# A four-layer hybrid decoder trunk on one core: the first two weight units split by halves, identity products before them, a padded input tensor, and three splits of weights in other places

## The chip, the cores and the metric

The kernel runs on one NeuronCore of one Trainium2 chip. TensorE (PE in the profile) multiplies, VectorE (DVE), ScalarE (ACT) and GpSimd (POOL) do the rest, and SyncE (SP) issues nearly all of the transfers. The metric is the device time of one execution in microseconds (us), as the median of several runs; lower is better.

## What is computed

256 tokens of width 1024 go through four layers. Each is a token mixer and an MLP, both behind an RMSNorm and with a residual. The mixers are latent attention (MLA, layers 0 and 3), block-sparse attention (MoBA, layer 1) and a Mamba-2 scan (SSD, layer 2).

```python
def reference(x, positions, ...):
    for i in range(4):
        h = rmsnorm(x, norm_mix[i])
        m = (mla_mixer, moba_mixer, ssd_mixer)[i % 3](h, ...)
        x = x + m
        x = x + sq_relu_mlp(rmsnorm(x, norm_mlp[i]), mlp_w1[i], mlp_w2[i])   # relu(h@w1)**2 @ w2
    return rmsnorm(x, norm_final)

def mla_mixer(h, positions, w_in, q_norm, w_uq, kv_norm, w_ukv, w_o):
    c_q, c_kv, k_pe = split(h @ w_in, [256, 512])            # w_in: 1024 x 576
    q = (rmsnorm(c_q, q_norm) @ w_uq)                        # 16 heads of 128 + 64
    k_nope, v = split(rmsnorm(c_kv, kv_norm) @ w_ukv)        # 16 heads of 128 + 128
    # rotary turn of q_pe and k_pe, causal softmax attention, then @ w_o
```

## The kernel before, in words

**Products in three parts.** Every fp32 operand is split into a high part (a rounded copy, type fp32r) and a low part (the value less its high part). A product a*b becomes three matmuls, a_hi*b_hi, a_hi*b_lo and a_lo*b_hi (`mm3`, lines 561 to 563). For the inputs the parts are `hhi` and `hlo`, both in the tile `hsplit`; for the weights they are `whi` and `wlo`. In the up-projections of the MLP (`pe_up`, lines 920 and 922) one matmul reads 512 columns, high and low part of `hsplit` side by side, and the next one 256.

**Weight units.** All weights come in 207 units of up to 128 x 2048 numbers (1 MB), in one fixed order (`units`), through four slots of `raw`, `whi` and `wlo`. SP loads unit n into `raw` (line 2075). ACT writes `whi` (`act_splits`, line 534), DVE writes `wlo` (`dve_splits`, line 544), and PE waits for that. SP may load slot s again when DVE has split it; ACT may write `whi` of slot s again when PE has used it. Each engine runs its own instruction list in program order; where in these lists the splits stand is written by hand: `act_splits(act, key, ahead)` and `dve_splits(dve, key, ahead)` emit all splits up to `ahead` units beyond `key`.

**The start.** The tokens are two tiles t = 0, 1 of 128. For each tile ACT sums the squares, DVE scales to a mean (`ms`, line 662), POOL takes the power -1/2 (`rstd`, line 745), DVE scales (`xn`, line 666), PE transposes (line 761), ACT writes `hhi` (line 611) and DVE `hlo` (line 688). Units 0 and 1 (the names `ca`, `cb` in `compress`) are the upper and lower half of the rows of the 1024 x 512 part of `w_in`; unit 2 holds the last 64 columns (`kpe`) and the first part of `w_uq`, unit 3 the first part of `w_ukv`, and units 4 and 5 the next parts of these two. PE runs `compress(0,0)`, then the transposes of tile 1, then `compress(1,0)`, `compress(0,1)` and `compress(1,1)`: 12 matmuls each, the first index is the unit, the second the tile. The latents that come out of them are normed too: ACT squares (`c_ssq`, line 1337), DVE `c_ms` (line 1382), POOL `c_rstd`, DVE writes the normed latents over `xn` (line 1389), and PE turns them (`turn(t)`, line 1256), with the 24 matmuls of `kpe` between the two turns. Behind the squares of tile 0, and in layer 0 alone, ACT computes the sines of the rotary angles (`act_angles`); DVE prepares them (`dve_turns`, `dve_angles`). Layer 3 goes the same way without the angles.

**The scan.** In the SSD layer a loop over q = 0 to 4 takes a quarter of the heads each. PE's products of unit ("z", 2q) write a bank that DVE must first have emptied in `scaled_inputs(q)` (line 1853); `state_inputs(q)` (line 1860) writes what PE multiplies between the units ("z", 2q) and ("z", 2q+1).

## Time and profile before

| | |
|---|---|
| median of 3 runs | 1342.49 us (1341.76 to 1343.81) |
| the profiled execution, its own time | 1342.94 us |
| span of its trace, first to last instruction | 1341.2 us |
| PE busy | 1300.3 us, 97% of the span, 7564 matmuls |
| DVE busy | 892.5 us, 67% |
| ACT busy | 671.7 us, 50% |
| mean granted TensorE clock | 0.993 |

A matmul's end is modelled, so each is shown longer than the distance to the next one's start, and an idle time that the profile gives for PE starts at such a modelled end. The distances between the starts are what the work takes. The chain is the sequence of work that ended last, followed back from the end.

### The profile page before, as it was taken

The numbers are of one execution on the slowest core, as the hardware profiler recorded it, in microseconds if no ns is written. First come the engines' busy times: TensorE is split into PE (matmuls) and PEld (weight loads), VectorE is DVE, ScalarE is ACT, GpSimd is POOL, SyncE is SP. The second block draws the span as 40 slices with busy tenths as digits, with TensorE's granted clock in tenths as the row PEclk, the third lists the DMA queues.
The fourth block names the chain that finished last, engine by engine and source line by source line (L and its number), as shares of the span: only waits on it lengthen the run. The fifth ranks groups of instructions, "written<-read, shape, count | busy, mean of one in ns | idle before, by whom it ended". The sixth has DMA issues, their size and how long they took to land.

```text
span 1341.2 us, 18335 instructions
## 1 busy us (share of the span) xinstructions
PE 1300.3 (97%) x7564; PEld 1132.1 (84%) x7564; DVE 892.5 (67%) x1179; ACT 671.7 (50%) x858; POOL 40.4 (3%) x58
## 2 busy tenths in 40 slices
PE   4999999999999999999999999999999999999998
PEld 3888888888899888887998988888887788888886
DVE  5777665555655566656898786666656876666664
ACT  4455454444455544444775554544444655454442
POOL 3000000000000000000101110000000000000000
PEclk9999999999999999999999999999999999999999
DMA  8653465555745475544564444655543343475540
GB/s 284 125 179 126 157 210 204 190 189 164 213 140 176 143 256 190 189 161 157 175 219 150 135 152 162 235 189 188 189 157 126 118 155 110 165 247 188 188 157 32
DMA packets 146067, 230.93 MB, mean 172 GB/s; under 512 B 7683, under 2 KB 112429, under 8 KB 145984
## 3 DMA queue, kind: packets, MB, share of 16 engines
q1 hardware_dynamic: 143136, 221.66, 49.5%
q0 software_dynamic: 2848, 8.10, 2.8%
q8 instruction: 61, 1.00, 0.3%
q14 instruction: 22, 0.18, 0.0%
HBM read 227.08 MB, written 2.65 MB: 171 GB/s over the span
## 4 chain that ended last, share of the span: by engine, by line
PE 85%; DVE 10%; ACT 2%; issue 2%; DMA 1%; POOL 0%; SPq 0%; POOLq 0%; DVEq 0%; ACTq 0%
PE bank L920 16%; PE acc L839 12%; PE acc L840 12%; PE acc L843 12%; PE bank L922 8%; PE bank L561 6%; PE bank L563 6%; PE bank L562 6%; DVE wlo L544 4%; DVE cacc L1823 2%; PE bank L1304 1%; PE bank L1039 1%; DMA raw<-in_mla_w_in 1%; ACT whi L534 1%; PE bank L1310 1%
## 5 line engine op out<-in xcount | busy, mean ns | idle before, releaser
L544 DVE TENSOR_TENSOR wlo<-raw,whi 128x2048 fp32r<-128x2048 f32 (+1 forms) x207 | 466.9, 2265 | 149.8 <-ACT whi L534 149.7
L534 ACT ACTIVATE whi<-raw 128x2048 fp32r<-128x2048 f32 (+1 forms) x207 | 388.4, 1888 | 49.9 <-PE acc L843 44.2
L920 PE MATMUL bank<-hsplit,whi 128*128 128x512 f32 x896 | 318.6, 398 | 0.0
L922 PE MATMUL bank<-hsplit,wlo 128*128 128x256 f32 x896 | 251.5, 281 | 0.0
L920 PEld LDWEIGHTS bank<-hsplit,whi 128*128 128x128 f32 x896 | 168.4, 188 | 41.2
L840 PE MATMUL acc<-wlo,uhi 128*128 128x512 f32 x512 | 200.0, 391 | 0.0
L839 PE MATMUL acc<-whi,uhi 128*128 128x512 f32 x512 | 199.6, 390 | 0.0
L922 PEld LDWEIGHTS bank<-hsplit,wlo 128*128 128x128 f32 x896 | 169.2, 189 | 2.2
L561 PE MATMUL bank<-hsplit,whi 128*128 128x256 f32 (+1 forms) x568 | 165.6, 292 | 5.5 <-DVE xn L1853 3.3
L563 PE MATMUL bank<-hsplit,wlo 128*128 128x256 f32 (+1 forms) x568 | 162.0, 285 | 0.0
L562 PE MATMUL bank<-hsplit,whi 128*128 128x256 f32 (+1 forms) x568 | 162.0, 285 | 0.0
L843 PE MATMUL acc<-whi,ulo 128*128 128x512 f32 x512 | 159.1, 389 | 0.0
L961 ACT ACTIVATE relu<-bank 128x512 f32<-128x512 f32 x56 | 33.4, 597 | 195.0 <-PE bank L922 195.0
L561 PEld LDWEIGHTS bank<-hsplit,whi 128*128 128x128 f32 (+1 forms) x568 | 108.6, 191 | 9.1 <-issue 8.8
L839 PEld LDWEIGHTS acc<-whi,uhi 128*128 128x128 f32 x512 | 96.1, 188 | 20.7
L843 PEld LDWEIGHTS acc<-whi,ulo 128*128 128x128 f32 x512 | 96.1, 188 | 20.4
L840 PEld LDWEIGHTS acc<-wlo,uhi 128*128 128x128 f32 x512 | 96.1, 188 | 18.1
L562 PEld LDWEIGHTS bank<-hsplit,whi 128*128 128x128 f32 (+1 forms) x568 | 108.5, 191 | 1.1 <-issue 1.0
L563 PEld LDWEIGHTS bank<-hsplit,wlo 128*128 128x128 f32 (+1 forms) x568 | 108.5, 191 | 0.2
L982 DVE TENSOR_TENSOR relu<-bank,relu 128x512 f32<-128x512 f32 x56 | 38.7, 691 | 101.7 <-ACT relu L961 101.7
L966 ACT ACTIVATE uhi<-rsq 128x512 fp32r<-128x512 f32 x64 | 40.5, 633 | 110.2 <-DVE rsq L984 81.5
L987 DVE TENSOR_TENSOR ulo<-rsq,uhi 128x512 fp32r<-128x512 f32 x64 | 44.3, 693 | 47.6 <-ACT uhi L966 47.6
(230 smaller groups left out, 1779.7 us busy)
## 6 DMA issues: line engine op xcount, KB each, us to landing
raw<-in_mlp_w SPq DMA_DIRECT2D x128, 1024.0 KB, 5.5
raw<-in_ssd_w_in SPq DMA_DIRECT2D x18, 1024.0 KB, 5.3
raw<-in_mla_w_o SPq DMA_DIRECT2D x16, 1024.0 KB, 4.8
raw<-in_mla_w_ukv SPq DMA_DIRECT2D x8, 1024.0 KB, 5.7
raw<-in_moba_w_qkv SPq DMA_DIRECT2D x16, 512.0 KB, 5.4
raw<-in_ssd_w_out SPq DMA_DIRECT2D x8, 1024.0 KB, 5.0
raw<-in_mla_w_uq SPq DMA_DIRECT2D x8, 768.0 KB, 5.4
raw<-in_mla_w_in SPq DMA_DIRECT2D x4, 1024.0 KB, 7.3
```

The lines of the kernel that those rows point to most:

```text
L534: nc.scalar.activation(whi[:, s, :e], raw[:, s, :e], ACT.Copy).then_inc(w_hi_done[s], 1)
L544: nc.vector.tensor_tensor(wlo[:, s, :e], raw[:, s, :e], whi[:, s, :e].bitcast(F32), ALU.subtract).then_inc(w_split[s], 1)
L561: nc.tensor.matmul(ps, lhs[0], rhs[0], start=start, stop=False)
L562: nc.tensor.matmul(ps, lhs[0], rhs[1], start=False, stop=False)
L563: return nc.tensor.matmul(ps, lhs[1], rhs[0], start=False, stop=stop)
L839: nc.tensor.matmul(acc[t][half][:], lh, wh[:, k, n], start=begin and k == 0, stop=False)
L840: nc.tensor.matmul(acc[t][half][:], lh, wl[:, k, n], start=False, stop=False)
L843: mm = nc.tensor.matmul(acc[t][half][:], ll, wh[:, k, n], start=False, stop=end and k == 1)
L920: nc.tensor.matmul(ps, w[0][:, k, n], hsplit[:, k].rearrange("p a n -> p (a n)"), start=k == 0, stop=False)
L922: mm = nc.tensor.matmul(ps[:, 0:SEQ], w[1][:, k, n], hhi[:, k, :], start=False, stop=k == KD - 1)
L966: nc.scalar.activation(uhi[:, c % 2].rearrange("p a b -> p (a b)"), rsq[:, c % 2, :], ACT.Copy).then_inc(uhi_done, 1)
L987: nc.vector.tensor_tensor(ulo[:, c % 2].rearrange("p a b -> p (a b)"), rsq[:, c % 2, :], uhi[:, c % 2].rearrange("p a b -> p (a b)").bitca ...
```

## The change

1. `hsplit` gets rows of 2 * 256 + 16 numbers in place of 2 * 256: its eight pieces lie 2112 bytes apart in place of 2048.
2. Units 0 and 1 are split in two halves each, on ACT and on DVE (`in_halves`, semaphores `half_hi_done` and `half_split`). PE starts on the first half and waits for the second in the middle of `compress`.
3. Behind the transposes of tile 0, PE runs seven fp32 products of `ident` with itself, 128 x 128, into an accumulator that is not in use.
4. DVE waits for the gains of the norm after `ms`, not ahead of it. It scales tile 1 ahead of the angles and of unit 1's split. ACT splits unit 1 ahead of tile 1's copies, and unit 2 after them.
5. In both MLA layers the splits of the next two units move. On ACT the first goes behind the squares of tile 0, the second behind the copy of the values `v_sb`; before, both stood behind `kpT`. On DVE the first goes behind the normed latents of tile 0, and the second takes the place where the first was.
6. In the SSD layer the last split of q = 0 on DVE goes behind `scaled_inputs(1)`.

```diff
-        hsplit = sb("hsplit", [P, KD, 2, SEQ], F32R)
+        hrows = sb("hsplit", [P, KD, 2 * SEQ + 16], F32R)
+        hsplit = hrows[:, :, 0:2 * SEQ].rearrange("p k (a n) -> p k a n", a=2)
...
+        in_halves = (0, 1) if kinds[0] == "mla" else ()
...
-                nc.scalar.activation(whi[:, s, :e], raw[:, s, :e], ACT.Copy).then_inc(w_hi_done[s], 1)
+                lo = 0
+                if n in in_halves:
+                    lo = e // 2
+                    nc.scalar.activation(whi[:, s, :lo], raw[:, s, :lo], ACT.Copy).then_inc(half_hi_done, 1)
+                nc.scalar.activation(whi[:, s, lo:e], raw[:, s, lo:e], ACT.Copy).then_inc(w_hi_done[s], 1)
...
+                if n in in_halves:
+                    lo = e // 2
+                    dve.wait_ge(half_hi_done, n + 1)
+                    nc.vector.tensor_tensor(wlo[:, s, :lo], raw[:, s, :lo], whi[:, s, :lo].bitcast(F32),
+                                            ALU.subtract).then_inc(half_split, 1)
...
                 if j == 0 and t == 1:
-                    act_splits(act, 2, 0)
+                    act_splits(act, 1, 0)
                 if j < len(stages):
                     act_tr(act, j, t)
                 if j == t == 0:
-                    act_splits(act, 0, 1)
+                    act_splits(act, 0, 0)
...
-            dve.wait_ge(gain_loaded, 16 * (j + 1))
             wait_x(dve, j, t)
             dve.wait_ge(ssq_done, c + 1)
             nc.vector.tensor_scalar(ms[:, c:c + 1], ssq[:, c:c + 1], 1.0 / DM, EPS, ALU.mult, ALU.add).then_inc(ms_done, 1)
+            dve.wait_ge(gain_loaded, 16 * (j + 1))
...
                 dve_splits(dve, 0, 0)
+                dve_scale_x(dve, j, 1)
                 dve_angles(dve)
                 dve_splits(dve, 0, 1)
-                dve_scale_x(dve, j, 1)
...
                 if t == 0:
-                    wait_unit(te, key)
+                    if halves:
+                        te.wait_ge(half_split, n + 1)
+                    else:
+                        wait_unit(te, key)
...
                 for k in range(KD // 2):
+                    if t == 0 and halves and k == KD // 4:
+                        wait_unit(te, key)
...
-                if t == 0 and j == 0:
-                    act_angles(act)
+                if t == 0:
+                    if j == 0:
+                        act_angles(act)
+                    act_splits(act, ("ukv", L, 0), 1)
...
             act_values(act, L, 0, 0)
+            act_splits(act, ("ukv", L, 0), 2)
...
-            act_splits(act, ("ukv", L, 0), AHEAD - 1)
...
             latents_normed(0)
+            dve_splits(dve, ("ukv", L, 0), 1)
             squares_scaled(1)
...
-            dve_splits(dve, ("ukv", L, 0), 1)
+            dve_splits(dve, ("ukv", L, 0), 2)
...
                 if 0 < q < 4:
                     scaled_inputs(q)
+                if q == 1:
+                    dve_splits(dve, ("z", 1))
...
-                    dve_splits(dve, ("z", 2 * q + 1))
+                    if q:
+                        dve_splits(dve, ("z", 2 * q + 1))
...
             pe_tr(te, 0, 0)
+            for _ in range(7):
+                nc.tensor.matmul(acc[0][0][:, 0:P], ident[:], ident[:], start=True, stop=True)
```

**First place: DVE's list in layer 0, from the latents' squares on.** `c_ms` and the `xn` rows that read a bank are the norm of the latents, `wlo` with 1536 numbers is the split of unit 4. Before:

```order
L544 TENSOR_TENSOR wlo<-raw,whi 128x2048 [waits w_hi_done2]
L544 TENSOR_TENSOR wlo<-raw,whi 128x2048 [waits w_hi_done3]
L1382 TENSOR_SCALAR c_ms<-c_ssq 128x2 [waits c_ssq_done_0,qkvg_loaded]
L1389 SCALAR_TENSOR_TENSOR xn<-bank,c_rstd,qkvg 128x256 [waits c_rstd_done_0]
L1389 SCALAR_TENSOR_TENSOR xn<-bank,c_rstd,qkvg 128x256
L1382 TENSOR_SCALAR c_ms<-c_ssq 128x2 [waits c_ssq_done_0]
L1395 TENSOR_TENSOR clo<-bank,chi 128x4x128 [waits c_hi_done_0]
L1389 SCALAR_TENSOR_TENSOR xn<-bank,c_rstd,qkvg 128x256 [waits c_rstd_done_0]
```

Now:

```order
L559 TENSOR_TENSOR wlo<-raw,whi 128x2048 [waits w_hi_done2]
L559 TENSOR_TENSOR wlo<-raw,whi 128x2048 [waits w_hi_done3]
L1405 TENSOR_SCALAR c_ms<-c_ssq 128x2 [waits c_ssq_done_0,qkvg_loaded]
L1412 SCALAR_TENSOR_TENSOR xn<-bank,c_rstd,qkvg 128x256 [waits c_rstd_done_0]
L1412 SCALAR_TENSOR_TENSOR xn<-bank,c_rstd,qkvg 128x256
L559 TENSOR_TENSOR wlo<-raw,whi 128x1536 [waits w_hi_done0]
L1405 TENSOR_SCALAR c_ms<-c_ssq 128x2 [waits c_ssq_done_0]
L1418 TENSOR_TENSOR clo<-bank,chi 128x4x128 [waits c_hi_done_0]
```

The split of unit 4 now stands between the two tiles' norms, so the norm of tile 1 and the turn of it on PE are behind it. The same piece stands in layer 3.

**Second place: ACT's list in layer 0, from tile 1's sum of squares (`junk,ssq`) to the copy of the turned latents (`chi`).** Before:

```order
L534 ACTIVATE whi<-raw 128x2048 [waits raw_loaded1]
L583 ACTIVATE junk,ssq<-x 128x1024 [waits ssq_done,x_loaded1]
L534 ACTIVATE whi<-raw 128x2048 [waits raw_loaded2]
L611 ACTIVATE hsplit<-bank 128x4x128 [waits bank_ready2]
L611 ACTIVATE hsplit<-bank 128x4x128 [waits bank_ready3]
L534 ACTIVATE whi<-raw 128x2048 [waits raw_loaded3]
```

Now:

```order
L598 ACTIVATE junk,ssq<-x 128x1024 [waits ssq_done,x_loaded1]
L542 ACTIVATE whi<-raw 128x1024 [waits raw_loaded1]
L543 ACTIVATE whi<-raw 128x1024
L626 ACTIVATE hsplit<-bank 128x4x128 [waits bank_ready2]
L626 ACTIVATE hsplit<-bank 128x4x128 [waits bank_ready3]
L543 ACTIVATE whi<-raw 128x2048 [waits raw_loaded2]
L543 ACTIVATE whi<-raw 128x2048 [waits raw_loaded3]
```

The sum of squares no longer waits for the load of unit 1, and unit 2's split went behind the copies of tile 1.

**Third place: DVE's list in the SSD layer, from the end of q = 0 to the start of q = 1.** The rows with `tokv` and `xn` are `scaled_inputs(1)`, `junk` are the results of q = 0, `gy` is the gate. Before:

```order
L1953 TENSOR_TENSOR junk<-bank,tokv 128x512 [waits bank_ready1]
L1959 TENSOR_TENSOR junk<-bank,junk 128x512 [waits bank_ready2,bank_free1]
L544 TENSOR_TENSOR wlo<-raw,whi 128x2048 [waits w_hi_done1]
L1853 TENSOR_TENSOR xn<-bank,tokv 128x512 [waits bank_ready3,dx_done]
L1853 TENSOR_TENSOR xn<-bank,tokv 128x512 [waits bank_ready0]
```

Now:

```order
L1979 TENSOR_TENSOR junk<-bank,tokv 128x512 [waits bank_ready1]
L1985 TENSOR_TENSOR junk<-bank,junk 128x512 [waits bank_ready2,bank_free1]
L1877 TENSOR_TENSOR xn<-bank,tokv 128x512 [waits bank_ready3,dx_done]
L1877 TENSOR_TENSOR xn<-bank,tokv 128x512 [waits bank_ready0]
L559 TENSOR_TENSOR wlo<-raw,whi 128x2048 [waits w_hi_done1]
```

The two rows that empty banks for PE now stand ahead of the split.

## Rows read from the trace of the kernel before

**Rows 1.** Who waited for whom on PE, whole span: us in total, times, longest

```profile
PE bank L761 <- DVE xn L666: 11.1, 2, 8.1
PE bank L561 <- DVE wlo L544: 5.8, 1, 5.8
```

**Rows 2.** Chain that ended last, first 60 us: start us, us, what

```profile
3.13 15.05 DMA raw<-in_mla_w_in
18.21 1.92 ACT whi L534
```

**Rows 3.** Timeline of DVE, layer 0: start us, us, operation, count, idle before

```profile
25.33 1.35 DVE L688 TENSOR_TENSOR hsplit<-bank,hsplit 128x512 fp32r<-128x512 f32 x2 [0.72 <-ACT hsplit L611]
...
27.06 4.47 DVE L544 TENSOR_TENSOR wlo<-raw,whi 128x2048 fp32r<-128x2048 f32 x2
31.46 0.15 DVE L1382 TENSOR_SCALAR c_ms<-c_ssq 128x2 f32<-128x2 f32 x1
32.46 0.88 DVE L1389 SCALAR_TENSOR_TENSOR xn<-bank,c_rstd,qkvg 128x256 f32<-128x256 f32 x2 [0.84 <-POOL c_rstd L1439]
...
47.36 1.76 DVE L544 TENSOR_TENSOR wlo<-raw,whi 128x1536 fp32r<-128x1536 f32 x1 [0.93 <-ACT whi L534]
```

**Rows 4.** Timeline of PE, layer 0

```profile
25.08 0.47 PE L561 MATMUL bank<-whi,hsplit 128*128 128x512 f32 x1
...
34.99 0.60 PE L1256 MATMUL bank<-ident,xn 128*128 128x128 f32 x4
...
38.23 0.66 PE L1256 MATMUL bank<-ident,xn 128*128 128x128 f32 x4
...
47.32 1.47 PE L1304 MATMUL bank<-kT,qT 128*128 128x128 f32 x8
```

**Rows 5.** Timeline of ACT, layer 0

```profile
24.70 1.26 ACT L611 ACTIVATE hsplit<-bank 128x512 fp32r<-128x512 f32 x2 [1.52 <-PE bank L761]
...
29.71 0.39 ACT L1337 ACTIVATE junk<-bank 128x256 f32<-128x256 f32 x1 [1.94 <-PE bank L563]
...
32.31 0.39 ACT L2035 ACTIVATE csn<-ang 128x64 f32<-128x64 f32 x2
```

**Rows 6.** Issue of unit 3's load (SP's timeline), and the DMA view of that issue

```profile
13.16 0.89 SPq L2075 DMA_DIRECT2D raw<-in_mla_w_ukv  x1
```

```profile
raw<-in_mla_w_ukv SPq DMA_DIRECT2D x1, 1024.0 KB, 10.6
```

**Rows 7.** Busy time by stretch, layers 0 and 3: PE, PEld, DVE, ACT, POOL, clock

```profile
59.30:64.90 5.60, 3.92 (x28) 3.09 (x26) 5.43 (x15) 3.47 (x12) 0.00 (x0) 1.00 0.75 150
1050.00:1056.30 6.30, 4.65 (x33) 3.80 (x32) 6.13 (x15) 3.48 (x12) 0.00 (x0) 1.00 0.47 166
```

**Rows 8.** Timelines of DVE and PE, layer 3

```profile
1025.54 0.88 DVE L1389 SCALAR_TENSOR_TENSOR xn<-bank,c_rstd,qkvg 128x256 f32<-128x256 f32 x2 [0.81 <-POOL c_rstd L1439]
```

```profile
1029.70 0.60 PE L1256 MATMUL bank<-ident,xn 128*128 128x128 f32 x4
```

**Rows 9.** Timelines of PE and DVE at q = 1 of the scan, and one stretch

```profile
727.29 0.36 PE L561 MATMUL bank<-hsplit,whi 128*128 128x256 f32 x1 [3.25 <-DVE xn L1853]
```

```profile
724.25 2.29 DVE L544 TENSOR_TENSOR wlo<-raw,whi 128x2048 fp32r<-128x2048 f32 x1 [1.38 <-ACT whi L534]
726.46 1.28 DVE L1853 TENSOR_TENSOR xn<-bank,tokv 128x512 f32<-128x512 f32 x2
...
731.06 0.68 DVE L1860 TENSOR_TENSOR xn<-xn,tokv 128x512 f32<-128x512 f32 x1
```

```profile
729.00:732.00 3.00, 3.00 (x16) 3.00 (x15) 2.96 (x6) 2.26 (x5) 0.72 (x2) 0.50 0.65 264
```

**Rows 10.** Timeline of PE in an MLP: eleven pairs L920 and L922, then twelve products

```profile
217.26 0.40 PE L920 MATMUL bank<-hsplit,whi 128*128 128x512 f32 x1
...
221.15 0.40 PE L839 MATMUL acc<-whi,uhi 128*128 128x512 f32 x1
...
223.90 0.39 PE L839 MATMUL acc<-whi,uhi 128*128 128x512 f32 x1
```

More of the change, by code:

```diff
@@ L153, in build @@
         xg_done = sem("xg_done")
+        half_hi_done = sem("half_hi_done")
+        half_split = sem("half_split")
         xn_upper_done = sem("xn_upper_done")
@@ L542, in dve_splits @@
                 e = units[n][0] * units[n][1]
+                lo = 0
+                if n in in_halves:
[3 more added lines that the diff above has]
+                                            ALU.subtract).then_inc(half_split, 1)
                 dve.wait_ge(w_hi_done[s], k + 1)
-                nc.vector.tensor_tensor(wlo[:, s, :e], raw[:, s, :e], whi[:, s, :e].bitcast(F32),
+                nc.vector.tensor_tensor(wlo[:, s, lo:e], raw[:, s, lo:e], whi[:, s, lo:e].bitcast(F32),
                                         ALU.subtract).then_inc(w_split[s], 1)
@@ L1237, in compress @@
                 key = (("ca", "cb")[n], L)
+                halves = first[key] in in_halves
                 if t == 0:
-                    wait_unit(te, key)
+                    if halves:
+                        te.wait_ge(half_split, n + 1)
+                    else:
+                        wait_unit(te, key)
                 ps = open_job(te, ("c", L, t)) if n == 0 else bank[jobs.at["c", L, t][0]]
```

## The prediction

> **What bounds the kernel now.** I read the page's busy times first: PE has work in 97% of the span, so time can only be won where PE waits, or where it works at half clock. The view of waits gives PE's idle time by cause; its two largest entries, 11.1 and 5.8 us [rows 1], both lie in the first 25 us. Next I read the chain: up to 18.2 us it is one transfer, unit 1's load, and then ACT's split of it [rows 2]. The timelines of PE, DVE and ACT from there on show who is late for whom, and two more kinds of place: in both MLA layers a stretch of some 6 us in which DVE is nearly always busy and PE is not [rows 7], and in the scan one wait of PE's of 3.3 us [rows 9]. Everywhere else PE's starts follow each other closely, and nothing that this change does there can help.
>
> **First weights (edits 2, 3, 4).** What stands ahead of unit 1's landing at 18.21 [rows 2] is worth nothing by itself: unit 0's halves bring PE's first products forward, but PE then waits for unit 1 anyway. The seven products of `ident` fit into the wait that PE has there, 5.8 us [rows 1], less the 2 us by which halving brings unit 0 forward (half of an ACT split of 1.92 and half of a DVE split of 2.24) [rows 2, 3]. An fp32 product costs, from the score products, 1.47 us for 768 columns [rows 4], so 0.25 us for 128 and 0.49 at half clock: 3.4 us at most, into 3.7. Were the cover gone, it would still be hidden behind the load. They cost nothing.
>
> From 18.21 on I count anew. ACT's halves end at 19.2 and 20.2; DVE's, each half of 2.24 and a little overhead, at 20.5 and 21.7. Tile 1's norm is by then long done, because DVE does it in the gap ahead of the load. It needs one sequence of small operation, POOL power and two DVE operations, and the latents' one of the same form takes 1.88 us (31.46 to 33.34) [rows 3]. So PE starts `compress(1,0)` at 20.6, not 25.08. The 36 products took 9.9 us [rows 4]; at the 0.229 us of a 512-column product at full clock [rows 10] they take 8.2, and the 1.7 between is a stretch at half clock (3.4 us long). They end at 28.8, or at 30.5 if the clock falls again.
>
> Now the others are late. ACT: the copies of tile 1 (1.26) [rows 5] to 21.5, unit 2's split to 23.4. Unit 3 lands at 13.16 + 10.6 = 23.8 [rows 6], so its split ends at 25.7. DVE: from 21.7 the low parts of tile 1 and the bias copy (1.73, from 25.33 to 27.06) [rows 3] to 23.4, unit 2 to 25.7, unit 3 from 25.85 to 28.1. Then the norm of the latents' tile 0, 1.88: 30.0. PE turns tile 0 at 30.05; it was 34.99. The new wait is the moved split of unit 4. On ACT it follows the squares and the sines (29.71 to 32.70, so 3.0) [rows 5]: 28.7, plus 1.5, is 30.2. On DVE it takes 1.76 [rows 3]: 32.05. Queued behind it are the second norm (1.88) and the turn of tile 1: 34.0. PE's own work up to there, turn and `kpe`, is 3.24 [rows 4] and would be done at 33.3, or at 33.8 after a fall of the clock. So the turn is at 34.0 in both cases; it was 38.23. That is 4.2 us less. POOL's seven small loads behind `rstd` of tile 1 now start while unit 1 to 3 are on their way; each delay of unit 3's landing delays the 34.0 by as much. I take 0.2 us for that, a choice, and keep 0 to 0.7: **-4.0**. The Trainium skill ("Trainium Kernel Development and Optimization", Key Constraints) says that transfers from the SP, ACT and POOL queues run on the same 16 DMA engines and interleave; by it the delay is not zero, and no row shows its size.
>
> **MLA, layer 0 (edit 5).** ACT's second moved split lies in an idle time of ACT. On DVE unit 5's split takes unit 4's old place, where DVE idled 0.93 [rows 3], and is 0.5 longer: no loss. The split that stood between the first normed probabilities and the next scores is gone there, 2.24 us out of the stretch from 59.3 to 64.9 in which DVE is busy for 5.43 of 5.6 us and PE idles 1.7 [rows 7]. A 256-column product is shown as 0.28 and takes 0.12 (24 of them in the 3.24 less the turn's 0.4) [rows 4], so four gaps hide 0.16 each: PE loses 1.7 to 2.3. All of it can come back, as DVE was 2.2 late. I take **-2.0**, and keep 1.0 to 2.3.
>
> **MLA, layer 3.** The same stretch, 1.65 idle by the same rows, returns 2.0. But here nothing at the front is won, and the wait stays: DVE ends the norm of tile 0 at 1026.4 [rows 8], then the moved split 1.76, then 1.88, is 1030.0, where PE turned tile 1 at 1029.70. That costs 0.3: **-1.7**.
>
> **Scan (edit 6).** Before unit ("z", 1)'s split DVE idles 1.38 us, waiting for ACT, with `scaled_inputs(1)` behind it [rows 9]. Its inputs are there, so it can run at 722.9 and end at 724.2. PE then goes on at 724.0 in place of 727.29: 3.3. The stretch of at least 3.0 us at half clock that follows the wait [rows 9] goes with it: 1.5. Then `state_inputs(1)` is late: the gates and it took from 727.7 to 731.7, now from 726.5 to 730.6, while PE ends its 48 products at 729.8. PE waits 0.8. Together **-4.0**; without a fall of the clock in both it is -2.5, which is the lower bound.
>
> **Padding (edit 1).** Copies into `hsplit` have rows of 128 numbers as before. What could change is PE's reading. A pair L920 and L922 takes 0.354 (3.89 for eleven), a 512-column product of the down-projection 0.229 (2.75 for twelve) [rows 10], and a 256-column one 0.12. So at most 5 to 6 ns of a pair could be the layout's, times 896 pairs, 5 us. In the trace the distances inside a chunk repeat in a cycle of three pairs, also where the second half of the chunk reads the same addresses again; that speaks of timing and not of addresses. I take 0. The skill ("TensorE: Matmul & The Clock Gate", the section on the 56 ns) has 215.7 ns start to start for 512 columns at full clock. By it a pair would be 325 ns, 28 ns less than here, and a layout that was to blame for all of it would hold 25 us. The down-projections, which do not read `hsplit`, are over that figure as well, so I keep to the rows. `ms` ahead of the gains (edit 4) wins some 0.3 us before the load and is hidden.
>
> **Sum.** 4.0 + 2.0 + 1.7 + 4.0 = 11.7. The profiled execution took 1342.94, so 1331.2; it stands 0.45 above the median, so the median should be 1330.8.
>
> **Rivals.**
> - *Part of it is hidden anyway.* The clock does not fall at q = 1 in most executions before either, and in MLA the next wait (ACT's copies of q and the turned tile) takes over after 1 us: 4.0 + 1.0 + 0.7 + 2.5 = 8.2, so 1334.3. For it: ACT and DVE are both in the chain there. Against: all three before times lie within 2 us. Chance 0.17.
> - *The padding helps.* Another 2 to 5 us: 1326 to 1329. The pairs are 6 ns longer than their parts elsewhere; the cycle of three speaks against it. 0.12.
> - *The start gives nothing.* Load of unit 3 or 4 is late, as DVE now asks for the units sooner and POOL's loads are ahead. ACT's split of unit 4 stands ahead of the squares of tile 1; if it landed after 28.7, everything behind it would wait. 4 us later and the 4.0 are gone: 1334.8. 0.08.
> - *No change or slower: the padded reads are slower.* PE reads `hsplit` in some 3,500 matmuls (1792 in L920 and L922, 568 each in the three lines of `mm3`). 3.3 ns more for each cancel the 11.7 us; 7 ns more give 1342.5 + 12.8 = 1355. Nothing in the trace speaks for it, but no row has padded tiles either. 0.03 slower, 0.03 in between.
> - My forecast: 0.57.
>
> **Range.** The measurement can tell about 0.2%, 2.7 us. The likeliest case alone spans 1328.5 to 1333: one stretch at half clock more or less, 1.7 us, in either kernel. With the partial case, the late load and the lesser half of the padding's help the range is 1326 to 1335.5. Faster 0.93, same 0.04, slower 0.03.
>
> **What the changed profile would show.** PE's first turn of latents at about 30.0 and the second at 34.0, with 0.7 us of idle time ahead of the second that ends with DVE; unit 3's ACT split starting at 23.8. None of PE's three waits between 55 and 60 and between 1038 and 1046. PE at q = 1 without the wait of 3.3 and without half clock, but with about 0.8 ahead of the product between the two z units. The pair L920 and L922 at 0.354. Wrong would be: a second turn much later than 34, from a late landing; the three waits in MLA still there, 2 us earlier; or a pair that differs from 0.354 by more than 2 ns, which is 1.8 us.

## The result and the profile after

The changed kernel takes 1324.24 us (median of four runs, 1323.87 to 1325.84), beside 1342.62 for the kernel before in the same comparison (1341.76 to 1343.81). The ratio is 0.9866, with a 95% interval of 0.9851 to 0.9882: 18.4 us faster, where 11.8 were forecast. 1324.2 lies below the range of 1326.0 to 1335.5. The sign and the places were right, the size was 6.6 us short.

I read the profile after in the order in which I had read the one before. First the page's busy times and the view of waits (us in total, times, longest):

```profile
PE 1292.8 (98%) x7578; PEld 1127.8 (85%) x7578; DVE 892.4 (67%) x1181; ACT 671.5 (51%) x860; POOL 40.3 (3%) x58
```

```profile
PE bank L776 <- DVE xn L681: 7.6, 1, 7.6
...
PE bank L576 <- DVE wlo L556: 1.9, 1, 1.9
PE bank L1277 <- DVE xn L1412: 1.2, 3, 0.5
PE bank L1684 <- DVE xn L1884: 0.9, 1, 0.9
```

PE is busy for 7.5 us less although it runs 14 matmuls more (the seven products of `ident`, each of which is two matmuls in the profile). Of my terms only the clock (3.2 us) makes PE less busy, the others were idle time; so a good part of the surplus must lie in the matmuls themselves. The waits are where they were expected: 5.8 at the first weights has become 1.9, and 0.9 in the scan (L1684) is new. The timeline of PE in layer 0 (start us, us, operation, idle before) gives the two turns, and that of DVE the moved split between the two norms of the latents:

```profile
14.40 0.79 PE L576 MATMUL bank<-whi,hsplit 128*128 128x512 f32 x1 [1.89 <-DVE wlo L556]
...
30.82 0.66 PE L1277 MATMUL bank<-ident,xn 128*128 128x128 f32 x4 [0.53 <-DVE xn L1412]
...
34.49 0.66 PE L1277 MATMUL bank<-ident,xn 128*128 128x128 f32 x4 [0.20 <-DVE xn L1412]
```

```profile
29.89 0.88 DVE L1412 SCALAR_TENSOR_TENSOR xn<-bank,c_rstd,qkvg 128x256 f32<-128x256 f32 x2 [0.85 <-POOL c_rstd L1463]
30.91 1.76 DVE L559 TENSOR_TENSOR wlo<-raw,whi 128x1536 fp32r<-128x1536 f32 x1
...
33.56 0.88 DVE L1412 SCALAR_TENSOR_TENSOR xn<-bank,c_rstd,qkvg 128x256 f32<-128x256 f32 x2 [0.22 <-POOL c_rstd L1463]
```

The turns were forecast at 30.05 and 34.0; they are at 30.82 and 34.49 (before: 34.99 and 38.23 [rows 4]). The stretches in MLA, the place of the old stretch at half clock behind an MLP (the row 339.00), and the start of the SSD layer (the row 626.00) by busy time and clock:

```profile
339.00:343.00 4.00, 3.64 (x31) 3.67 (x32) 1.63 (x4) 1.36 (x4) 2.35 (x3) 1.00 0.24 25
626.00:634.00 8.00, 6.33 (x41) 5.65 (x42) 2.87 (x7) 2.94 (x4) 0.00 (x0) 0.79 0.00 1
53.50:59.00 5.50, 5.32 (x45) 5.09 (x43) 5.33 (x15) 3.48 (x12) 0.00 (x0) 1.00 0.47 48
1032.50:1038.80 6.30, 6.11 (x50) 5.83 (x48) 6.09 (x18) 3.48 (x12) 0.00 (x0) 1.00 0.00 0
```

In MLA, PE is now busy for 5.32 of 5.5 and 6.11 of 6.3 us, where it was 3.92 of 5.6 and 4.65 of 6.3 [rows 7]. The other two rows answer to these two of the kernel before, which I had not looked at:

```profile
346.00:350.00 4.00, 3.86 (x20) 3.89 (x21) 1.41 (x3) 1.05 (x3) 2.35 (x3) 0.57 0.28 36
636.00:644.00 8.00, 6.22 (x32) 5.38 (x33) 2.98 (x7) 2.47 (x4) 0.00 (x0) 0.57 0.00 1
```

The first is a stretch at half clock that the changed kernel does not have; in the second it is twice as long before (6.8 us) as after (3.4). At q = 1 of the scan the timelines of PE and DVE show the forecast order, and the new wait of 0.9:

```profile
720.02 1.13 PE L1684 MATMUL bank<-xn,Btok 128*128 128x512 f32 x2 [0.91 <-DVE xn L1884]
```

```profile
712.23 1.29 DVE L1877 TENSOR_TENSOR xn<-bank,tokv 128x512 f32<-128x512 f32 x2
713.68 2.29 DVE L559 TENSOR_TENSOR wlo<-raw,whi 128x2048 fp32r<-128x2048 f32 x1 [0.16 <-ACT whi L543]
...
719.29 0.68 DVE L1884 TENSOR_TENSOR xn<-xn,tokv 128x512 f32<-128x512 f32 x1
```

Last the MLP, two starts of a down-projection chunk, with 24 matmuls of it and the 32 of an up-projection between them. Before and after:

```profile
221.15 0.40 PE L839 MATMUL acc<-whi,uhi 128*128 128x512 f32 x1
...
232.26 0.40 PE L839 MATMUL acc<-whi,uhi 128*128 128x512 f32 x1
```

```profile
214.97 0.40 PE L854 MATMUL acc<-whi,uhi 128*128 128x512 f32 x1
...
226.01 0.40 PE L854 MATMUL acc<-whi,uhi 128*128 128x512 f32 x1
```

11.11 us have become 11.04, and nearly all chunks are alike (11.107 and 11.047 as medians; in the changed kernel the first one of each MLP takes 0.1 us more). From the first to the last product of the chunks the four MLPs take 664.7 us before and 661.8 after, which is 2.9 us less. The shown durations of the matmuls hardly differ (0.40 and 0.39); only the distances between starts tell it. A pair of 512 and 256 columns takes 352.5 ns before and 348.0 after, as the mean over all 896.

**What to explain.** To compare places, I take the start of the same matmul in both traces. It is earlier by 3.75 us behind the second turn of layer 0, by 5.96 at 66 us, by 10.96 at 711, 14.82 at 832, 15.40 at 1045, 17.60 at 1066, and 18.6 at the end. The moves stand for 3.75 + 2.2 + 3.85 + 2.0, which is 11.8 (layer 3 gains 2.2 at 1045 us and has lost 0.25 at its second turn). The other 6.8 us are gained in places where no work was moved.

### The profile page after: what moved, and what is told of

Its sections match the earlier page's. It is cut to its first block, busy times and chain, and to the rows that moved or that the text cites. A ratio compares the mean times of both kernels' runs of the same rounds, so it can differ in the third digit from the quotient of the medians.

```text
span 1322.6 us, 18369 instructions
## 1 busy us (share of the span) xinstructions
PE 1292.8 (98%) x7578; PEld 1127.8 (85%) x7578; DVE 892.4 (67%) x1181; ACT 671.5 (51%) x860; POOL 40.3 (3%) x58
## 4 chain that ended last, share of the span: by engine, by line
PE 84%; DVE 10%; ACT 2%; issue 2%; SPq 1%; DMA 1%; POOL 0%; POOLq 0%; DVEq 0%; ACTq 0%
PE bank L935 16%; PE acc L854 12%; PE acc L855 12%; PE acc L858 12%; PE bank L937 8%; PE bank L576 6%; PE bank L578 5%; PE bank L577 5%; DVE wlo L559 4%; DVE cacc L1847 2%; PE bank L1325 1%; ACT whi L543 1%; PE bank L1054 1%; SPq L2102 1%; PE bank L1331 1%
## 5 line engine op out<-in xcount | busy, mean ns | idle before, releaser
L559 DVE TENSOR_TENSOR wlo<-raw,whi 128x2048 fp32r<-128x2048 f32 (+2 forms) x207 | 464.7, 2255 | 141.3 <-ACT whi L543 141.0
L543 ACT ACTIVATE whi<-raw 128x2048 fp32r<-128x2048 f32 (+2 forms) x207 | 387.0, 1880 | 45.5 <-PE acc L858 44.7
L935 PE MATMUL bank<-hsplit,whi 128*128 128x512 f32 x896 | 314.0, 392 | 0.0
L576 PE MATMUL bank<-hsplit,whi 128*128 128x256 f32 (+1 forms) x568 | 163.2, 287 | 3.1 <-DVE hsplit L703 1.5
L577 PE MATMUL bank<-hsplit,whi 128*128 128x256 f32 (+1 forms) x568 | 160.3, 282 | 0.0
L855 PEld LDWEIGHTS acc<-wlo,uhi 128*128 128x128 f32 x512 | 96.0, 188 | 18.5
L576 PEld LDWEIGHTS bank<-hsplit,whi 128*128 128x128 f32 (+1 forms) x568 | 106.0, 187 | 6.5 <-issue 6.2
L577 PEld LDWEIGHTS bank<-hsplit,whi 128*128 128x128 f32 (+1 forms) x568 | 105.5, 186 | 1.1 <-issue 1.0
```

Source lines behind the costliest of these rows:

```text
L543: nc.scalar.activation(whi[:, s, lo:e], raw[:, s, lo:e], ACT.Copy).then_inc(w_hi_done[s], 1)
L559: nc.vector.tensor_tensor(wlo[:, s, lo:e], raw[:, s, lo:e], whi[:, s, lo:e].bitcast(F32), ALU.subtract).then_inc(w_split[s], 1)
L576: nc.tensor.matmul(ps, lhs[0], rhs[0], start=start, stop=False)
L577: nc.tensor.matmul(ps, lhs[0], rhs[1], start=False, stop=False)
L855: nc.tensor.matmul(acc[t][half][:], lh, wl[:, k, n], start=False, stop=False)
L935: nc.tensor.matmul(ps, w[0][:, k, n], hsplit[:, k].rearrange("p a n -> p (a n)"), start=k == 0, stop=False)
```

## The experiments

The theories: **A**, PE's distance between matmuls depends on the addresses of what it reads, and the padding wins about 5 us that way. **B**, as I had forecast, the padding is worth nothing and the moves are worth more. **C**, the terms add up. **D**, the clock follows the edits. **E**, what slows PE's reading is the other engines' traffic. **F**, the same addresses have more than one pattern. Times are medians beside the kernel before on the same chip, which took 1342.0 to 1343.2.

**1. One part of the change at a time, on the kernel before.** The padding alone:

```diff
-        hsplit = sb("hsplit", [P, KD, 2, SEQ], F32R)
+        hrows = sb("hsplit", [P, KD, 2 * SEQ + 16], F32R)
+        hsplit = hrows[:, :, 0:2 * SEQ].rearrange("p k (a n) -> p k a n", a=2)
```

> The kernel before with the padded rows of hsplit as its only change. Theory A (addresses: the distance between starts of matmuls that read hsplit depends on how far its pieces lie apart): the pair takes about 0.348 us in place of 0.354, the products of mm3 that read it some 1 to 2 ns less each, together 5 to 7 us less, so about 1336.5. Theory B (what I predicted: the cycle of three is one of timing, and the shorter pairs in the changed kernel come from its other edits): pair 0.354, time 1342.5 within 1. In neither does PE wait anywhere else.

1336.42 us (1335.87 to 1338.55), ratio 0.9955 [0.9942, 0.9967]: 6.4 us faster. A pair takes 348.0 ns. B falls. Some of the 6.4 is clock: its five runs had a mean granted clock of 0.9942, the kernel before 0.9930, and 0.0012 of 1342 us is 1.6.

The changed kernel with these lines reversed:

> The changed kernel with the rows of hsplit back at 2048 bytes. Theory A: pairs at 0.354 again, 5 to 7 us slower than the changed kernel, 1329.5 to 1331.5, which is what I had forecast for a padding worth nothing. Theory B: 1324.2 as with the padding, and the moves of work are worth more than I had counted.

1329.18 (1328.35 to 1329.89): 4.9 us slower than the changed kernel, pairs at 352.5 again. It is also 1.6 us below my forecast, with a padding worth nothing in both.

The scan alone (edit 6) and the moved splits in MLA alone (edit 5):

> The kernel before with edit 6 (the scan) alone. My term: 4.0 us less, 1338.5, with the wait of 3.25 us at q = 1 gone, PE at full clock there, and a new wait of 0.8 us between the two z units. Rival: the clock falls somewhere else in its place, then 2.5 us less, 1340.0.

1338.82 over eleven runs, ratio 0.997 [0.9961, 0.9979]: 4.0 us. Its runs spread from 1336.1 to 1341.5 with granted clocks of 0.996 to 0.992, so single stretches at half clock come and go. In the profiled execution the same matmuls are 0.2 us early at 711 us and 4.3 early at 832.

> The kernel before with edit 5 (the splits in both MLA layers) alone. In layer 3 my term of 1.7 us less holds, perhaps 2.0 as the changed kernel shows. In layer 0 without the earlier start the same three waits go (2.0 less), while the second turn of latents waits for a split more. Sum 3.5 to 4.0 less, so about 1338.8. Rival: PE's stretches at half clock at 346 and 637 us in the kernel before belong to waits that this edit does not touch; they stay. If they are gone, they are luck of one execution or depend on what ran long before.

1337.62, ratio 0.9958 [0.9945, 0.997]: 5.2 us. The trace gives 2.2 in layer 0 and 2.2 in layer 3, less 0.25 for the later turn there: 4.15. The other 1.1 is clock: the profiled execution has no stretch at half clock at 346 us, which is worth 1.5, and is 0.3 us later at the start. It has the one of 6.8 us at 637, as the kernel before has.

The start alone (edits 2, 3 and 4):

> The kernel before with edits 2, 3 and 4 alone (halves, identity products, the new order at the start). The turn of tile 1 has no moved split ahead of it here, so it could come at about 33.3 in place of 34.0, and the 4.0 us of my term become 4.7 by then; at the end of layer 0 what is left is 3.7 to 4.7. Theory C (terms add up): the rest of the program shifts by that and the time is 1338 to 1339. Theory D (clock): the stretch at half clock at 25 us goes as well, since PE has the identity products, and it is inside that number; if further stretches go, at 637 and 729 us, which this edit does not touch, the time is 1336 to 1337.

1338.11, ratio 0.9965 [0.9952, 0.9977]: 4.9 us. The second turn is at 33.74, since no split stands ahead of it, and from there on all is 4.5 us early. PE falls to half clock here in places without any edit, at 341.5 and at 1007 us (us, busy times, clock):

```profile
341.50:345.50 4.00, 3.87 (x20) 3.90 (x21) 1.40 (x3) 1.04 (x3) 2.35 (x3) 0.58 0.30 40
1007.00:1011.00 4.00, 3.51 (x9) 2.77 (x10) 1.76 (x4) 1.41 (x4) 0.55 (x1) 0.59 0.04 12
```

The two places follow a norm, where PE waits for about 1.9 us in every kernel of this study. The stretch at half clock behind the wait at q = 1 of the scan [rows 9] is missing here, and PE gains 1.5 us by it, though this edit does not touch the scan and the wait of 3.2 us is still there. The four parts alone add up to 20.5 us, 2.1 more than the change. So C holds to within 2.1 us, and some of these are counted more than once: three of the four profiles (padding, scan, MLA) lack the 1.5 us of the stretch at 346 us.

**2. The identity products.** The changed kernel without the seven matmuls:

```diff
-            for _ in range(7):
-                nc.tensor.matmul(acc[0][0][:, 0:P], ident[:], ident[:], start=True, stop=True)
```

> The changed kernel without the seven identity products. My step: they cost nothing, because unit 1's load covers them: 1324.2 within 1. Theory D: they keep PE's clock up; without them the stretch at half clock near 25 us comes back, and with it up to 1.7 us of the start: 1326.

1324.66, ratio 0.9866 [0.9851, 0.988]: no difference. The stretch at half clock near 25 us, which the kernel before has, does not come back, so the products neither cost nor bring anything that can be seen in the time, and D falls for them:

```profile
14.00:29.00 15.00, 14.58 (x56) 10.90 (x57) 12.70 (x21) 10.21 (x14) 4.19 (x8) 1.00 1.00 338
```

The clock of 1.00 in this row must not be read as full speed from 14 us on: the trace's first record of the clock is at 18.4 us (at 20.4 in the changed kernel). Up to there the 512-column products start 427 ns apart, about twice the 230 ns of later, so PE begins at half clock in both. It is at full clock from 18.5 us without the seven products and from 20.8 us with them; they did not bring it up sooner.

**3. Which address?** Other spacings, by 8 and 24 numbers in place of 16:

> The changed kernel with pieces 2080 bytes apart (8 numbers of padding in place of 16). Theory A (any spacing other than 2048 breaks the cycle): pair 0.348 as with 64 bytes, 1324. Theory A3 (the gain grows with the spacing, or wants multiples of 64 bytes): pair between 0.348 and 0.354, 1325 to 1329.

1327.73; a pair takes 350.3 ns on the mean.

> The changed kernel with pieces 2144 bytes apart (24 numbers). Theory A: pair 0.348, 1324. Theory A3: a pair shorter than 0.348 (if the gain grows) or back towards 0.354 (if multiples of 64 matter), 1322 to 1329.

1325.11; a pair takes 347.3, but the first of the down-projection's three products (line 854) 230.7 ns in place of 228.7. So the gain has no simple course with the spacing. The 64 bytes once, ahead of the tile:

```diff
-        hrows = sb("hsplit", [P, KD, 2 * SEQ + 16], F32R)
-        hsplit = hrows[:, :, 0:2 * SEQ].rearrange("p k (a n) -> p k a n", a=2)
+        hrows = sb("hsplit", [P, KD * 2 * SEQ + 16], F32R)
+        hsplit = hrows[:, 16:].rearrange("p (k a n) -> p k a n", k=KD, a=2)
```

> The changed kernel with the same 64 bytes added once, ahead of the whole tile, in place of once per piece: the pieces lie 2048 bytes apart again, each 64 bytes later. Theory A (what counts is that the eight pieces start at different offsets): pairs at 0.354 in the cycle of three, 1329.2 as without the padding. Theory A2 (what counts is the offset itself, and the old one was unlucky): pairs at 0.348 or less, 1324.

1336.73: neither of the two, but 7.5 us slower than with no shift. The pairs stay at 352.2; the down-projection, which doesn't read `hsplit`, went from 228 to 233.7 ns a matmul. Its stationary operands `uhi` and `ulo` are allocated behind `hsplit` and had moved by 64 bytes as well. The same with the 64 bytes behind the tile (`hrows[:, 0:KD * 2 * SEQ]`), so that `hsplit` lies where it was:

> The changed kernel with the 64 bytes behind hsplit: hsplit itself lies as in the kernel before, and everything allocated behind it, the stationary uhi and ulo of the down-projections among them, 64 bytes later. Theory A4 (what made the run with the 64 bytes ahead of hsplit slow is the new offset of the stationary operands): the down-projections' products take 233 ns in place of 228, as there, the pairs 0.3525 again; 1536 of these and 480 output products at 5.6 ns more are 11 us, on top of 1329.2: about 1339 to 1340. Rival: it was the offset of hsplit, the moving operand: 1329.

1334.21, 5.0 us slower than with no shift. Two starts of a chunk, and the first product of the pairs between them:

```profile
215.64 0.39 PE L854 MATMUL acc<-whi,uhi 128*128 128x512 f32 x1
...
221.24 0.39 PE L935 MATMUL bank<-hsplit,whi 128*128 128x512 f32 x1
...
226.79 0.39 PE L854 MATMUL acc<-whi,uhi 128*128 128x512 f32 x1
```

The down-projection's 24 matmuls take 5.60 us in place of 5.47, so the stationary operand's address matters. But the 32 of the up-projection take 5.55 in place of 5.64, and none of their operands has moved. That was in no theory: I had expected 1339. Last, all of the kernel before moved by 384 bytes, with an unused tile ahead of the first:

```diff
+        lead = sb("lead", [P, 96])
         raw = sb("raw", [P, SLOTS, UNIT])
```

> The kernel before with an unused tile of 384 bytes ahead of all others, so that the large operands start at a multiple of 512 bytes, in place of 128 beyond one. If a matmul's distance depends on the absolute offset, all of them change, by 0 to 10 ns each: 1325 to 1350. If only the offset of one operand against the other counts, nothing changes: 1342.8.

1341.9, ratio 0.9995 [0.9986, 1.0004], and the same pairs of 352.5: a shift of 384 bytes that is common to all operands does not count. Here too the wait at q = 1 (3.2 us) has no stretch at half clock behind it.

**4. PE alone.** The matmuls on zeros, with no other engine at work; the network is left out.

```python
for i in range(48): nc.tensor.matmul(ps[:, i % 2, :], station(128, i), moving(128, 2048, i), start=True, stop=True)
```

> No part of the network: PE alone runs blocks of 48 matmuls of 512 columns on zeros, each with a new stationary piece, while nothing else reads or writes the tiles; the output is zeros. In the blocks the start of the moving pieces and of the stationary pieces takes six offsets each (0, 32, 64, 128, 256, 384 bytes beyond a multiple of 512), then the spacing of the moving pieces changes from 2048 to 2080, 2112, 2144 and 2176 bytes, then pairs of 512 and 256 columns as in the up-projection. Theory A (PE's own reading depends on the addresses): the distance between starts differs by 3 to 14 ns between blocks, in the same way as in the kernels (236 ns at 2048 against 230 at 2112, for pairs 354 against 348). Theory E (the other engines' traffic to the same memory makes it, and the addresses decide who meets whom): all blocks have the same distance, at or below the 226 ns that is the least seen in the kernels.

The timeline of PE has a row for each block. In the rows below the stationary pieces start 128 bytes beyond a multiple of 512, and the moving ones 64, 128, 256 and 384; the row at 299.69 shows where the fourth block ends:

```profile
255.50 11.36 PE L82 MATMUL ps<-mv,st 128*128 128x512 f32 x48
266.69 11.06 PE L83 MATMUL ps<-mv,st 128*128 128x512 f32 x48
277.60 11.35 PE L84 MATMUL ps<-mv,st 128*128 128x512 f32 x48
288.79 11.06 PE L85 MATMUL ps<-mv,st 128*128 128x512 f32 x48
299.69 11.05 PE L86 MATMUL ps<-mv,st 128*128 128x512 f32 x48
```

From start to start a block of 48 takes 11.19, 10.91, 11.19 and 10.90 us: about 233 and 227 ns a matmul. Of the 36 combinations, the ten whose two offsets are equal or differ by 256 bytes come out at 226.6 to 226.9 once the start of the block is past; all others lie between 228.9 and 234.3. So E falls: PE alone shows differences of the size that the kernels have. A spacing of 2112 bytes is worse for such a sequence (231.7 against 226.7); it is better only for pairs of 512 and 256 columns (349.2 ns a pair against 353.3, from start to start of the blocks).

The up-projection's own sequence:

> No part of the network: PE alone runs the matmul pattern of the up-projection on zeros (512 columns with a piece of whi, then 256 with a piece of wlo, eight pieces of the input, two output halves, three slots), 48 pairs a block; the output is zeros. From block to block the start of the input pieces (0, 32, 64, 128, 192 bytes), the padding between them (0, 32, 64, 96) and the start of wlo (0, 32, 64, 128, 192) change, and in the last four blocks the order of the matmuls. Theory A (the addresses of moving and stationary pieces set the distance): a pair takes 353 to 354 ns with no padding and 348 with 64 bytes, as in the kernels, and some combination is below 348, perhaps near 340 (1.5 times the 226.7 of matched offsets). Theory E (in the kernels it is the other engines' traffic as well): with PE alone the padding makes no difference of more than 1 ns a pair.

Theory A was half right: 64 bytes of padding gave 349.1, but no padding gave 346.7, and not 353. So I put the down-projection's matmuls ahead, at the kernels' addresses.

> No part of the network: PE alone runs, on zeros, the 24 matmuls of a down-projection chunk and the 32 of an up-projection chunk with every operand at the address that it has in the kernels, three chunks a block; the output is zeros. The blocks differ in the padding of the input tile (0, 32, 64, 96 bytes), in the offset of all that lies behind it (0, 32, 64, 128, 192), of the input tile too, and of wlo. Theory A (addresses, with PE alone): the chunk's time comes out as in the kernels: pairs of 352.5 with no padding and 348 with 64 bytes, the down-projection at 228, and 231 to 236 when uhi and ulo lie 64 bytes later. Theory F (a second thing that the last two runs suggest: with no padding the same addresses have two patterns, 346.7 and 352.5 ns a pair, and the matmuls ahead of the pairs decide which one PE falls into): with no padding the pairs change from 352.5 to about 347 when only the down-projection's operands ahead of them move.

Each full row is three chunks. The first three rows are the layout before, and that with `uhi` and `ulo` 32 and 64 bytes later; then the layout of the changed kernel, and one with `wlo` and all behind it 64 bytes later and no padding:

```profile
78.77 33.49 PE L77 MATMUL ps<-big 128*128 128x512 f32 x168
112.09 33.73 PE L78 MATMUL ps<-big 128*128 128x512 f32 x168
145.66 33.61 PE L79 MATMUL ps<-big 128*128 128x512 f32 x168
179.11 1.09 PE L80 MATMUL ps<-big 128*128 128x512 f32 x4
...
413.53 33.30 PE L87 MATMUL ps<-big 128*128 128x512 f32 x168
446.66 1.55 PE L88 MATMUL ps<-big 128*128 128x512 f32 x6
...
1248.31 33.16 PE L112 MATMUL ps<-big 128*128 128x512 f32 x168
1281.30 9.06 PE L113 MATMUL ps<-big 128*128 128x512 f32 x43
```

From start to start the layout before takes 33.32 us, so 11.11 a chunk, and the changed kernel's 33.13, so 11.04. That is what the two kernels take. With `uhi` and `ulo` 64 bytes later it is 33.45, so 11.15, as in the run with the 64 bytes behind the tile. The last layout takes 32.99 (11.007 for the second and for the third of its chunks). The distances agree one by one: without padding 227, 113, 232, 118, 241, 120 ns, with it 227, 113, 227, 118, 232, 117, in this run and in the kernels. With no padding the pairs are 352.6 on the mean when `uhi` lies as before and 347.1 when it lies 64 bytes later, although no operand of the pairs has moved. Both A and F hold. Why PE's reading depends on these offsets, no run shows.

**5. Is it a forecast?** Two layouts that no kernel had yet. First `wlo` and all behind it 64 bytes later, with no padding:

```diff
+        between = sb("between", [P, 16])
         wlo = sb("wlo", [P, SLOTS, UNIT], F32R)
```

> The changed kernel without any padding in hsplit, but with an unused tile of 64 bytes between whi and wlo, so that wlo, hsplit, uhi and all behind them lie 64 bytes later against whi. With PE alone a chunk of this layout took 11.01 us (pairs 342.7 ns, down-projection 230.3), the padded one 11.04 (347.6 and 228.3), the one without padding 11.11. Theory A: the profile shows the same distances, the MLPs are 0.03 us a chunk faster than in the changed kernel, 56 chunks, 1.7 us, so 1322.5, give or take what the other stages' matmuls do at the new offsets (up to 5 ns on some 2,500 matmuls, 10 us, either way). Rival: in the kernel, with the other engines at work, the pairs are not at 343.

1323.58 (1323.10 to 1324.28), forecast 1322.5, but with up to 10 us either way for the other stages. It is 0.7 us below the changed kernel, which is within the noise, so the time alone confirms nothing. The chunk does, with 11.01 us:

```profile
215.37 0.39 PE L854 MATMUL acc<-whi,uhi 128*128 128x512 f32 x1
...
226.38 0.39 PE L854 MATMUL acc<-whi,uhi 128*128 128x512 f32 x1
```

Then 79 layouts with PE alone (80 blocks, one layout stands twice), and the best of them in the kernel: `hsplit` 160 bytes later as a whole, 96 unused bytes behind it, no padding.

> No part of the network: the blocks with PE alone once more, for 80 layouts: wlo 0 to 224 bytes later, the input tile 0 to 224 bytes later in steps of 32, padding of 0 to 96; the output is zeros. Theory A expects no layout below 227 ns for 512 columns and 113 for 256, so no chunk below 24 times 226.7 and 16 times 340, 10.88 us; the best is between that and 11.01.

The least was 11.00 us a chunk, and none came near 10.88.

```diff
+        hrows = sb("hsplit", [P, KD * 2 * SEQ + 64], F32R)
+        hsplit = hrows[:, 40:40 + KD * 2 * SEQ].rearrange("p (k a n) -> p k a n", k=KD, a=2)
```

> The changed kernel without padding between the pieces, but with hsplit as a whole 160 bytes later and 96 unused bytes behind it, so that uhi, ulo and the rest keep their offsets. The layout came out best with PE alone: 11.00 us a chunk (pairs 347.4, down-projection 226.8) against 11.04 for the padded one. By that the MLPs are 0.04 us a chunk faster, 2.2 us in 56 chunks: 1322.0. Rival: the other stages' matmuls that read hsplit are slower at this offset (up to 3 ns on 1700 matmuls, 5 us): 1324 to 1327.

1322.74 (1321.30 to 1324.41), ratio to the kernel before 0.985 [0.9836, 0.9863], and 11.00 us a chunk in its trace:

```profile
215.18 0.39 PE L854 MATMUL acc<-whi,uhi 128*128 128x512 f32 x1
...
226.18 0.39 PE L854 MATMUL acc<-whi,uhi 128*128 128x512 f32 x1
```

It is the fastest version, 1.5 us below the changed kernel, but their intervals overlap, and 1.5 us is less than this measurement can tell. For the chunk, PE alone and the kernel agree within 0.01 us in all eight layouts that ran both ways. In the kernels (medians) the layout before takes 11.107 us, the 64 bytes behind the tile 11.153, ahead of it 11.247, spacings of 2080, 2112 and 2144 bytes 11.080, 11.047 and 11.047, and the last two layouts 11.007 and 11.000. With PE alone they take 11.11, 11.15, 11.25, 11.08, 11.05, 11.05, 11.01 and 11.00 once the first chunk of a block is past. Only for the last two was the number there before the kernel ran.

## Why the forecast fell short

| term | forecast | measured, by the same matmuls in the traces |
|---|---|---|
| start of layer 0 | 4.0 | 3.75 (alone 4.5, with no split ahead of the second turn) |
| MLA, layer 0 | 2.0 | 2.2 |
| MLA, layer 3 | 1.7 | 2.0 |
| scan, q = 1 | 4.0 | 3.85 (alone 4.1), 1.5 of it a stretch at half clock |
| padding | 0 | 4.9 (undone), 6.4 (alone, with about 1.6 of clock) |
| identity products, halves, `ms` | 0 | the products 0.4, within the noise; the others not tried alone |
| clock elsewhere | 0 | about 1 |

**The step that failed is the padding, "I take 0".** It was bounded rightly (5 us at most), and "the padding helps" (2 to 5 us, chance 0.12) named the cause and nearly the size. Its times of 1326 to 1329 were not reached, because the clock gave more as well. The prediction's own sign of being wrong, a pair more than 2 ns off 0.354, came out. The argument that chose between the bounds was wrong: the distances "repeat in a cycle of three pairs, also where the second half of the chunk reads the same addresses again; that speaks of timing and not of addresses". The observation is right, and the runs show why it proves nothing. A pattern has a state that the matmuls ahead leave behind, and each layout has its own set of patterns. With the same operands, the pairs take 352.5 or 347 ns by what ran before them, and with 64 bytes of padding about 348. The sum also bounded the wrong set: `mm3` reads `hsplit` as well. Of the 4.9 us, 2.9 come from the MLPs (664.7 us less 661.8): their 896 pairs gain 4.0, and their down-projections lose 1.2 (228.6 ns a matmul in place of 227.8). The rest, 2.0, I put down to `mm3`, whose three lines with `hsplit` and 256 columns sum to 211.0 us from start to start without the padding and 208.3 with it (a part of that difference is clock); no run tried it apart. The prediction's count of some 3,500 products that read `hsplit` also leaves out the 288 of `compress` that read it as the moving operand.

**The clock is the smaller part.** Without the padding the changed kernel is at 1329.2, 13.4 us below the kernel before, where I had 11.8. The moves explain next to nothing of the 1.6: MLA gave 0.5 more than forecast, the start and the scan 0.4 less, together 11.8 against 11.7. In the profile of this kernel the surplus is one stretch at half clock, the one at 346 us, worth 1.5. The mean granted clock was 0.993 in the 55 runs of the kernel before beside the experiments, and 0.996 in the four of this one; (0.007 times 1342) less (0.004 times 1329) is 4.1 us, of which my terms counted 3.2. I had counted only stretches at half clock that follow a wait which the change removes. The one at 346 us in the kernel before is in that profile by chance: of the 14 other kernels, all with the same wait there, only one has it. The one behind the wait at q = 1, 1.5 of my 4.0 us for the scan, is no sure thing either: of the five profiled kernels that still have that wait (3.2 or 3.3 us), three show it and two don't. That this part of the sum came out is partly luck; the exchange of the wait of 3.3 us for one of 0.9 is not. What makes the clock fall in one execution and not in another, and why the changed kernel has fewer, stays open.

**Right, by its own steps:** the order at the start, the moved split between the two norms (its late turn came 0.5 us later than forecast, with 0.20 of idle time in place of 0.7), the three waits in MLA gone in both layers, the later turn in layer 3 (0.25 against 0.3), the wait of 3.3 at q = 1 replaced by 0.9 (0.8 forecast), and the products of `ident` free. The rival that part of it is hidden anyway is out, apart from its doubt about the clock at q = 1. So is the one of slow padded reads, though it was nearer than I thought: moving the same 64 bytes to one side of the tile costs 5 to 7.5 us.

## What to carry to other kernels

When a kernel is bound by TensorE, measure the distance between starts in the inner loop, and try offsets of a few dozen bytes between its stationary and moving operands; any new tile moves all that are allocated behind it, so an edit elsewhere can gain or lose 5 us in this way, and a comparison should keep the addresses or check the distances. The loop's matmuls alone, on zeros and at the real addresses, gave the kernel's chunk within 0.01 us, and some 80 layouts fit into one run. They tell the chunk and not the kernel: with the 64 bytes behind `hsplit`, 56 chunks at 0.046 us more are 2.6 of the 5.0 us. A regular cycle in the distances does not exclude the addresses as its cause.

## What the runs showed of the hardware that was not expected

- With nothing else at work, 512-column matmuls with a new stationary piece each stand 226.7 ns apart where moving and stationary pieces start at matching offsets, and 228.9 to 234.3 otherwise. The ten matching combinations of the 36 are those whose offsets are equal or differ by 256 bytes. In a kernel, moving everything together by 384 bytes changed nothing.
- The same pairs of matmuls, with the same operands, take 352.6 or 347.1 ns on the mean by the matmuls ahead of them. At best a pair took 340.0 (with `wlo` 64 bytes later, second half of the chunk).
- The Trainium skill ("TensorE: Matmul & The Clock Gate", the section on the 56 ns) has 215.7 ns from start to start for 512 columns at full clock. The trace does not agree for these fp32r products, each with a new stationary piece: no sequence here had a mean below 226.6.
